# Where the blocks of x are added up for the layer norms at the ends of out, att_out and pool_out

## The chip, the cores and the metric

One core of one Trainium2 chip runs the whole program. The metric is device microseconds from start to end of one execution; the times shown are the median, lowest and highest of three runs. Durations inside the program come from one profiled execution.

## The reference, cut to what matters

A token matrix x of 256 tokens by 1024 channels passes through two transformer-like blocks (a gated mixer with a state-space branch and a squared-ReLU MLP; then attention, a pooling mixer and four gated MLPs). Eight times the new x is formed from a matrix product and normed before the next stage:

```
x = x + g1 * (mixed @ w_out)                       # "out", then h2 = rms_norm(x) * (1 + sc2) + sh2
x = x + g2 * (square(relu(h2 @ w_ff1)) @ w_ff2)    # "ff2", then rms_norm(x, final_norm_w)
x = layer_norm(ALPHA * x + 0.5 * swiglu(x) @ down)  # "down0", "down1", "down2", "down3"
x = layer_norm(ALPHA * x + attention(x) @ w_out)    # "att_out"
x = layer_norm(ALPHA * x + pool_mixer(x) @ w_out)   # "pool_out"
```

layer_norm needs the mean and the mean square over the 1024 channels of each token, rms_norm the mean square alone.

## The kernel before, in words

All data is fp32. x lies transposed in SBUF (tile `XS`): eight blocks of 128 channels by 256 tokens, each beside its square (`xb` is the x half, `sq` the square half), so `XS[:, m, :, :]` is 128x512. Weights come as 1 MB panels of 128x2048 into four slots of `raw`, by a DMA from SP's queue (`refill`), which waits until VectorE has split the panel that lay there. A panel is split in two halves of 128x1024: ScalarE rounds it into `w_hi` (L1104), VectorE subtracts to get `w_lo` (L1504), two panels ahead of TensorE. A product is then three matmuls (w_lo by the rounded operand, w_hi by the operand's rest, w_hi by the rounded operand: L601, L603, L604).

Each of the stages above has two groups of four output blocks. VectorE takes a block up out of PSUM and makes the new x of it (`new_x`: L1565 in out and ff2, L1560 elsewhere); ScalarE squares it (four blocks at once at L1156 for the first group, one by one at L1112 for the last). The last group is finished bank by bank (`each=bank_done`), so that its four takes can follow the matmuls closely (`last_group`, `bank_post`).

For the norm TensorE multiplies by a constant matrix `mean_w` of 1/1024, which sums over the partitions; the eight blocks are added up beforehand as far as possible. GpSimd adds blocks 0 to 4, with their squares, into `part` (`add_first_group`, L567: four adds), VectorE adds block 5 (`add_block`, L1573) ahead of the take of block 7, its last, and TensorE takes blocks 6 and 7 by themselves (`stats`, L747 to L757: three matmuls for the mean, three for the mean square; out and ff2 have only the last three). VectorE then computes the variance (L1618, or L1621 without a mean), ScalarE the inverse root, and the normed blocks `H` are made one by one for the next stage's first products (`apply_norm`, with two half-panel splits in between).

The order on each engine is the order of the code. Stages with 8 input blocks go through `run`: in out and pool_out VectorE and ScalarE split both halves of the next stage's first panel before the last group's takes. att_out is written out by hand: a loop over 14 half panels (`for i in range(14)`) splits, among others, the first panel of gu1 in its last two turns, then the takes of both groups follow.

## Time and profile before

| | us |
| --- | --- |
| median of 3 runs | 1671.67 |
| lowest, highest | 1669.38, 1672.41 |
| the profiled execution | 1670.81 |
| its span, first to last instruction | 1668.9 |
| TensorE matmul busy | 1584.6 (95%) |
| VectorE busy | 997.2 (60%) |
| ScalarE busy | 770.9 (46%) |
| GpSimd busy | 185.7 (11%) |

The profiled execution took 1.9 us more than its span. "PE" is TensorE's matmuls, DVE VectorE, ACT ScalarE, POOL GpSimd, SPq the queue from which SP issues DMAs. In a timeline a row gives the start, the duration, the engine, the line, the operation with output and inputs, how many were merged into the row, and in brackets how long the engine had been idle before and what it waited for. In a row of windows come the stretch and its length, the busy time of TensorE's matmuls, its weight loads, VectorE, ScalarE and GpSimd, and then the granted clock of TensorE (1.00 is 2.4 GHz, 0.50 is 1.2 GHz, between them a mean of both), the DMA share and GB/s. The mean granted clock over the span is 0.968.

### The profile page before, as it was taken

Reading aid. Unit: us, or ns where it says so; the run is one execution under the profiler, and the core shown is the slowest. Engines: PE = TensorE matmul, PEld = TensorE weight load, DVE = VectorE, ACT = ScalarE, POOL = GpSimd, SP = SyncE. Lnnn points to the kernel's source line nnn. Section 1 sums busy time; section 2 is a strip of 40 time slices with the busy share of each in tenths; the row PEclk is TensorE's granted clock in tenths of the full one; section 3 lists DMA queues with packets and bytes.
Section 4 is the critical chain, followed back from the end, with each engine's and each line's share of the span. In section 5 each row is a group of like instructions: output and inputs, shape, how many; then the busy total and the mean of one; then the engine's idle time right before and its main releaser. Section 6 shows DMA issues by size and latency. Waiting matters only on the chain.

```text
span 1668.9 us, 30136 instructions
## 1 busy us (share of the span) xinstructions
PE 1584.6 (95%) x12512; PEld 1534.6 (92%) x12512; DVE 997.2 (60%) x1278; ACT 770.9 (46%) x1006; POOL 185.7 (11%) x143
## 2 busy tenths in 40 slices
PE   7999999988999999999999879999999997799997
PEld 5999998878989999999989679999899997799997
DVE  5876894345766645655465655555655558565545
ACT  3544555444455534544443545443544444354433
POOL 0100002332110001000022012001200013120001
PEclk9999999989999999999999989999999998899999
DMA  8964763222535555455535325554455543344550
GB/s 316 368 246 165 292 229 124 102 77 102 185 145 179 191 185 177 163 190 176 187 141 189 114 79 200 178 194 181 151 179 187 190 177 127 126 152 176 180 192 32
DMA packets 42153, 289.66 MB, mean 174 GB/s; under 512 B 4843, under 2 KB 7019, under 8 KB 7500
## 3 DMA queue, kind: packets, MB, share of 16 engines
q1 hardware_dynamic: 41244, 284.44, 46.9%
q0 software_dynamic: 816, 3.87, 0.6%
q8 instruction: 72, 1.18, 0.3%
q14 instruction: 21, 0.17, 0.0%
HBM read 285.15 MB, written 3.15 MB: 173 GB/s over the span
## 4 chain that ended last, share of the span: by engine, by line
PE 86%; DVE 6%; ACT 3%; issue 2%; POOL 1%; DMA 1%; SPq 0%; ACTq 0%; POOLq 0%; DVEq 0%
PE banks L601 21%; PE banks L603 21%; PE banks L604 20%; PE banks L702 6%; PE banks L704 6%; PE banks L705 6%; DVE w_lo L1504 2%; ACT w_hi L1104 1%; POOL part L567 1%; PE banks L916 0%; PE banks L733 0%; PE banks L827 0%; DMA raw<-in_panels 0%; PE banks L919 0%; PE banks L826 0%
## 5 line engine op out<-in xcount | busy, mean ns | idle before, releaser
L1504 DVE TENSOR_TENSOR w_lo<-raw,w_hi 128x1024 fp32r<-128x1024 f32 x490 | 614.5, 1263 | 532.1 <-ACT w_hi L1104 526.9
L1104 ACT ACTIVATE w_hi<-raw 128x1024 fp32r<-128x1024 f32 x490 | 515.4, 1057 | 578.7 <-PE banks L604 421.4
L601 PE MATMUL banks<-H,w_lo 128*128 128x256 f32 x1920 | 549.5, 286 | 29.6 <-DVE H L1644 20.1
L603 PE MATMUL banks<-H,w_hi 128*128 128x256 f32 x1920 | 548.3, 286 | 0.0
L604 PE MATMUL banks<-H,w_hi 128*128 128x256 f32 x1920 | 546.6, 285 | 0.0
L601 PEld LDWEIGHTS banks<-H,w_lo 128*128 128x128 f32 x1920 | 368.7, 192 | 32.8 <-issue 32.3
L604 PEld LDWEIGHTS banks<-H,w_hi 128*128 128x128 f32 x1920 | 369.1, 192 | 0.0
L603 PEld LDWEIGHTS banks<-H,w_hi 128*128 128x128 f32 x1920 | 369.1, 192 | 0.0
L603 PE MATMUL banks<-HH,w_hi 128*128 128x256 f32 x960 | 270.8, 282 | 0.0
L601 PE MATMUL banks<-HH,w_lo 128*128 128x256 f32 x960 | 270.6, 282 | 0.0
L604 PE MATMUL banks<-HH,w_hi 128*128 128x256 f32 x960 | 270.1, 281 | 0.0
L702 PE MATMUL banks<-H,w_lo 128*128 128x256 f32 x640 | 188.3, 294 | 3.8 <-DVE H L1707 3.6
L704 PE MATMUL banks<-H,w_hi 128*128 128x256 f32 x640 | 185.4, 290 | 0.0
L705 PE MATMUL banks<-H,w_hi 128*128 128x256 f32 x640 | 185.1, 289 | 0.0
L604 PEld LDWEIGHTS banks<-HH,w_hi 128*128 128x128 f32 x960 | 181.0, 189 | 0.0
L603 PEld LDWEIGHTS banks<-HH,w_hi 128*128 128x128 f32 x960 | 180.8, 188 | 0.0
L601 PEld LDWEIGHTS banks<-HH,w_lo 128*128 128x128 f32 x960 | 180.7, 188 | 0.0
L702 PEld LDWEIGHTS banks<-H,w_lo 128*128 128x128 f32 x640 | 125.9, 197 | 6.4 <-issue 6.0
L704 PEld LDWEIGHTS banks<-H,w_hi 128*128 128x128 f32 x640 | 126.0, 197 | 0.0
L705 PEld LDWEIGHTS banks<-H,w_hi 128*128 128x128 f32 x640 | 125.7, 196 | 0.0
L567 POOL TENSOR_TENSOR part<-XS 128x512 f32<-128x512 f32 x8 | 10.3, 1289 | 904.4 <-issue 582.8
L1134 ACT ACTIVATE HH<-ev 128x512 f32 (+2 forms) x52 | 36.3, 698 | 80.6 <-DVE ev L1549 67.8
(285 smaller groups left out, 1706.5 us busy)
## 6 DMA issues: line engine op xcount, KB each, us to landing
raw<-in_panels SPq DMA_DIRECT2D x269, 1024.0 KB, 4.8
bias_rows<-rev POOLq DMA_DIRECT2D x1, 2048.0 KB, 16.9
XS<-in_x_t SPq DMA_DIRECT2D x1, 1024.0 KB, 6.6
near<-bias_rows POOLq DMA_DIRECT2D x8, 128.0 KB, 2.8
out_t<-XS SPq DMA_DIRECT2D x4, 256.0 KB, 2.6
ws<-in_ws_t POOLq DMA_DIRECT2D x1, 512.0 KB, 9.3
cols<-in_cols SPq DMA_DIRECT2D x1, 180.0 KB, 2.4
wdt<-in_wdt POOLq DMA_DIRECT2D x1, 128.0 KB, 5.9
```

Source lines behind the costliest of these rows:

```text
L567: pool.tensor_tensor(total, XS[:, 0, :, :] if b == 1 else total, XS[:, b, :, :], ALU.add)\
L601: pe.matmul(acc, w_lo[:, panel_slot, at:at + P], operand[:, kk, 0, :], start=starts and c == chunks[0], stop=False)
L603: pe.matmul(acc, w_hi[:, panel_slot, at:at + P], operand[:, kk, 1, :], start=False, stop=False)
L604: return pe.matmul(acc, w_hi[:, panel_slot, at:at + P], operand[:, kk, 0, :], start=False, stop=stops and c == chunks[-1])
L702: pe.matmul(acc, w_lo[:, q % SPLIT, at:at + P], operand[:, k, 0, :], start=p == 0 and c == 0 and b % 2 == 0, stop=False)
L704: pe.matmul(acc, w_hi[:, q % SPLIT, at:at + P], operand[:, k, 1, :], start=False, stop=False)
L705: last = pe.matmul(acc, w_hi[:, q % SPLIT, at:at + P], operand[:, k, 0, :], start=False, stop=p == panels - 1 and c == 3 and b % 2 == 1)
L1104: act.activation(w_hi[:, sl, w], raw[:, r, w], ACT.Copy).then_inc(panel_hi, 1)
L1134: act.activation(view[:, g, :, :], ev[:, G, 0:blocks, :], ACT.Copy).then_inc(operand_hi, 1)
L1504: vec.tensor_tensor(w_lo[:, sl, w], raw[:, r, w], w_hi[:, sl, w], ALU.subtract).then_inc(panel_lo, 1)
```

## The change

At three of the eight ends (out, att_out, pool_out) GpSimd no longer adds; VectorE adds all of blocks 1 to 5 to block 0. `SUMMED_AHEAD` names the five other ends, where GpSimd's adds stay.

- out and pool_out: VectorE makes the first three adds right behind the first group's takes (each waits for the one before it), splits only half 0 of the next panel, takes two blocks, adds block 4, takes, adds block 5, takes the last block, and then splits half 1.
- att_out: VectorE's loop has 12 turns in place of 14, so the two halves of gu1's first panel are split behind the last take and the last add. The first group's takes release ScalarE one by one (`x_early`), and ScalarE squares them one by one. The adds stand between the last group's takes, that of block 5 behind the last.
- TensorE, at all ends but att_out: the product with `part` comes first, ahead of blocks 6 and 7. At att_out it comes behind them, but ahead of the square of block 7.
- ScalarE's splits, and the order of the DMAs, are not moved.

VectorE's rows at the end of att_out. L1504 (before) and L1524 (after) are the splits, L1560 and L1583 the takes, L1573 and L1598 the adds, L1608 and L1652 the first step of the norm. Before:

```order
L1504 TENSOR_TENSOR w_lo<-raw,w_hi 128x1024
L2003 TENSOR_TENSOR AO<-banks,AO 128x256 x2
L1504 TENSOR_TENSOR w_lo<-raw,w_hi 128x1024 x2
L1560 SCALAR_TENSOR_TENSOR XS<-XS,banks 128x256 x7
L1573 TENSOR_TENSOR part<-part,XS 128x512
L1560 SCALAR_TENSOR_TENSOR XS<-XS,banks 128x256
L1608 TENSOR_TENSOR XS<-XS,banks 128x256
```

After:

```order
L2044 TENSOR_TENSOR AO<-banks,AO 128x256 x2
L1583 SCALAR_TENSOR_TENSOR XS<-XS,banks 128x256 x5
L1598 TENSOR_TENSOR part<-XS 128x512
L1598 TENSOR_TENSOR part<-part,XS 128x512
L1583 SCALAR_TENSOR_TENSOR XS<-XS,banks 128x256
L1598 TENSOR_TENSOR part<-part,XS 128x512
L1583 SCALAR_TENSOR_TENSOR XS<-XS,banks 128x256
L1598 TENSOR_TENSOR part<-part,XS 128x512
L1583 SCALAR_TENSOR_TENSOR XS<-XS,banks 128x256
L1598 TENSOR_TENSOR part<-part,XS 128x512
L1524 TENSOR_TENSOR w_lo<-raw,w_hi 128x1024 x2
L1652 TENSOR_TENSOR XS<-XS,banks 128x256
```

The two splits went from ahead of the eight takes to behind them, and five adds stand where one was.

VectorE's rows at the end of pool_out (out has the same order). Before:

```order
L1560 SCALAR_TENSOR_TENSOR XS<-XS,banks 128x256 x4
L1504 TENSOR_TENSOR w_lo<-raw,w_hi 128x1024 x2
L1560 SCALAR_TENSOR_TENSOR XS<-XS,banks 128x256 x3
L1573 TENSOR_TENSOR part<-part,XS 128x512
L1560 SCALAR_TENSOR_TENSOR XS<-XS,banks 128x256
L1608 TENSOR_TENSOR XS<-XS,banks 128x256
```

After:

```order
L1583 SCALAR_TENSOR_TENSOR XS<-XS,banks 128x256 x4
L1598 TENSOR_TENSOR part<-XS 128x512
L1598 TENSOR_TENSOR part<-part,XS 128x512 x2
L1524 TENSOR_TENSOR w_lo<-raw,w_hi 128x1024
L1583 SCALAR_TENSOR_TENSOR XS<-XS,banks 128x256 x2
L1598 TENSOR_TENSOR part<-part,XS 128x512
L1583 SCALAR_TENSOR_TENSOR XS<-XS,banks 128x256
L1598 TENSOR_TENSOR part<-part,XS 128x512
L1583 SCALAR_TENSOR_TENSOR XS<-XS,banks 128x256
L1524 TENSOR_TENSOR w_lo<-raw,w_hi 128x1024
L1652 TENSOR_TENSOR XS<-XS,banks 128x256
```

Three adds stand ahead of the split, two between the takes, and one half of the split went behind the last take.

TensorE's rows for the statistics of down0 (down1, down2, down3 and pool_out have the same). `part` is the sum of blocks 0 to 5. Before:

```order
L747 MATMUL banks<-XS,mean_w 128x256
L749 MATMUL banks<-XS,mean_w 128x256
L751 MATMUL banks<-part,mean_w 128x256
L753 MATMUL banks<-XS,mean_w 128x256
L755 MATMUL banks<-part,mean_w 128x256
L757 MATMUL banks<-XS,mean_w 128x256
```

After:

```order
L753 MATMUL banks<-part,mean_w 128x256
L759 MATMUL banks<-XS,mean_w 128x256
L761 MATMUL banks<-XS,mean_w 128x256
L753 MATMUL banks<-part,mean_w 128x256
L767 MATMUL banks<-XS,mean_w 128x256
L772 MATMUL banks<-XS,mean_w 128x256
```

The product with `part` went from third place to first, so that behind the take of block 7 (which L749 and L761 wait for) four matmuls follow and no longer five.

The diff, cut to its core:

```diff
@@ -94,2 +94,5 @@
 
+
+SUMMED_AHEAD = tuple(n for n in NORMED if n not in ("out", "att_out", "pool_out"))
+
 COUNTED = {
...
@@ -557,2 +560,3 @@
                 k = n - 2
+                done = BANKS * SUMMED_AHEAD.index(NORMED[k])
                 pool.wait_ge(taken, FIRST_GROUP[INDEX[NORMED[k]]] + 1)
...
@@ -563,3 +567,3 @@
                     if b > 1:
-                        pool.wait_ge(S["norm_part"], 4 * k + b - 1)
+                        pool.wait_ge(S["norm_part"], done + b - 1)
                     if b >= BANKS:
...
@@ -580,3 +582,4 @@
                         .then_inc(S["pool_lo_wide"], 1)
-                add_first_group(4 + i)
+                if NORMED[i + 2] in SUMMED_AHEAD:
+                    add_first_group(4 + i)
 
...
@@ -744,15 +747,27 @@
                     mean_at, square_at = banks[:, b, 0:T], banks[:, b + 1, 0:T]
+                    late = stage == "att_out"
+
+                    def whole(at, i, start):
+
+                        pe.wait_ge(S["norm_whole"], k + 1)
+                        return pe.matmul(at, mean_w[:, :], part[:, i, :], start=start, stop=i == 0 and not start)
+
                     pe.wait_ge(bank_x, (BANKS - 1) * (k + 1))
                     if mean:
-                        pe.matmul(mean_at, mean_w[:, :], xb[:, KD - 2, :], start=True, stop=False)
+                        if not late:
+                            whole(mean_at, 0, True)
+                        pe.matmul(mean_at, mean_w[:, :], xb[:, KD - 2, :], start=late, stop=False)
                         pe.wait_ge(taken, FIRST_GROUP[INDEX[stage] + 1])
-                        pe.matmul(mean_at, mean_w[:, :], xb[:, KD - 1, :], start=False, stop=False)
-                        pe.wait_ge(S["norm_whole"], k + 1)
-                        pe.matmul(mean_at, mean_w[:, :], part[:, 0, :], start=False, stop=True)                            .then_inc(S["mean_sum"], 1)
+                        last = pe.matmul(mean_at, mean_w[:, :], xb[:, KD - 1, :], start=False, stop=not late)
+                        if not late:
+                            last.then_inc(S["mean_sum"], 1)
+                    if not late:
+                        whole(square_at, 1, True)
                     pe.wait_ge(S["squares"], KD * n + KD - 1)
-                    pe.matmul(square_at, mean_w[:, :], sq[:, KD - 2, :], start=True, stop=False)
-                    pe.wait_ge(S["norm_whole"], k + 1)
-                    pe.matmul(square_at, mean_w[:, :], part[:, 1, :], start=False, stop=False)
+                    pe.matmul(square_at, mean_w[:, :], sq[:, KD - 2, :], start=late, stop=False)
+                    if late:
+                        whole(mean_at, 0, False).then_inc(S["mean_sum"], 1)
+                        whole(square_at, 1, False)
                     pe.wait_ge(S["squares"], KD * (n + 1))
-                    pe.matmul(square_at, mean_w[:, :], sq[:, KD - 1, :], start=False, stop=True)                        .then_inc(S["stat_sums"], 1)
+                    pe.matmul(square_at, mean_w[:, :], sq[:, KD - 1, :], start=False, stop=True).then_inc(S["stat_sums"], 1)
                     return
...
@@ -1467,4 +1482,9 @@
                     exps(h)
-            for g in range(2):
-                squares_post(INDEX["att_out"], g, (att_group + g) % 2)
+            for b in range(BANKS):
+                if b < BANKS - 1:
+                    act.wait_ge(S["x_early"], b + 1)
+                else:
+                    act.wait_ge(taken, FIRST_GROUP[INDEX["att_out"]] + 1)
+                act.activation(sq[:, b, :], xb[:, b, :], ACT.Square).then_inc(S["squares"], 1)
+            squares_post(INDEX["att_out"], 1, 1 - att_group)
             layer_norm("att_out")
...
@@ -1572,3 +1595,9 @@
                 vec.wait_ge(S["squares"], KD * (k + 2) + m + 1)
-                vec.tensor_tensor(part[:, :, :], part[:, :, :], XS[:, m, :, :], ALU.add).then_inc(S["norm_whole"], 1)
+                if m == 1:
+                    vec.wait_ge(S["stat_sums"], k + 2)
+                ins = vec.tensor_tensor(part[:, :, :], XS[:, 0, :, :] if m == 1 else part[:, :, :], XS[:, m, :, :], ALU.add)
+                if m == 5:
+                    ins.then_inc(S["norm_whole"], 1)
+                else:
+                    step(ins)
 
...
@@ -1576,7 +1605,17 @@
 
-                for b in range(BANKS):
-                    if b == BANKS - 1:
-                        vec.wait_ge(S["norm_part"], 4 * NORMED.index(name) + 4)
-                        add_block(name, 5)
-                    bank_post(INDEX[name], g, G, b, new_x)
+                alone = name in SUMMED_AHEAD
+                adds = {3: (5,)} if alone else {1: (1, 2), 2: (3,), 3: (4,), 4: (5,)} if name == "att_out" else {2: (4,), 3: (5,)}
+                for b in range(BANKS + 1):
+                    if b == BANKS - 1 and alone:
+                        vec.wait_ge(S["norm_part"], BANKS * SUMMED_AHEAD.index(name) + BANKS)
+                    for m in adds.get(b, ()):
+                        add_block(name, m)
+                    if b < BANKS:
+                        bank_post(INDEX[name], g, G, b, new_x)
+
+            def split_but_last(name):
+
+                def split_some(q, *place, halves=(0, 1)):
+                    split(q, *place, halves=(0,) if q == FIRST_PANEL[INDEX[name] + 1] else halves)
+                return split_some
 
...
@@ -1589,2 +1628,4 @@
                         last_group(name, g, G, new_x)
+                        if name not in SUMMED_AHEAD:
+                            split_half(FIRST_PANEL[s + 1], 1)
                         return
...
@@ -1594,3 +1635,6 @@
                     last.then_inc(taken, 1)
-                run(vec, INDEX[name], split, take_up)
+                    if name not in SUMMED_AHEAD:
+                        for m in (1, 2, 3):
+                            add_block(name, m)
+                run(vec, INDEX[name], split if name in SUMMED_AHEAD else split_but_last(name), take_up)
 
...
@@ -2005,3 +2046,3 @@
 
-            for i in range(14):
+            for i in range(12):
                 q, half = att_half(i)
...
@@ -2017,5 +2058,6 @@
             for b in range(BANKS):
-                last = deep_x(b, banks[:, NEAR + b // 2, b % 2 * T:b % 2 * T + T])
-            last.then_inc(taken, 1)
+                deep_x(b, banks[:, NEAR + b // 2, b % 2 * T:b % 2 * T + T]).then_inc(taken if b == BANKS - 1 else S["x_early"], 1)
             last_group("att_out", 1, 1 - att_group, deep_x)
+            split_half(att_half(12)[0] + SPLIT, 0)
+            split_half(att_half(12)[0] + SPLIT, 1)
             layer_norm("att_out", 1)
```

## Rows read from the trace of the kernel before

**Rows 1.** The page: the chain that ended last, by engine.

```profile
PE 86%; DVE 6%; ACT 3%; issue 2%; POOL 1%; DMA 1%; SPq 0%; ACTq 0%; POOLq 0%; DVEq 0%
```

**Rows 2.** Timeline of TensorE, end of att_out (start us, us, engine, line).

```profile
979.82 0.28 PE L604 MATMUL banks<-AO,w_hi 128*128 128x256 f32 x1
...
989.35 0.61 PE L757 MATMUL banks<-XS,mean_w 128*128 128x256 f32 x2
993.38 0.55 PE L601 MATMUL banks<-H,w_lo 128*128 128x256 f32 x1 [3.42 <-DVE H L1644]
```

**Rows 3.** Timeline of VectorE there.

```profile
975.53 1.23 DVE L1504 TENSOR_TENSOR w_lo<-raw,w_hi 128x1024 fp32r<-128x1024 f32 x1 [1.56 <-ACT w_hi L1104]
976.68 2.46 DVE L1560 SCALAR_TENSOR_TENSOR XS<-XS,banks 128x256 f32<-128x256 f32 x7
984.70 0.69 DVE L1573 TENSOR_TENSOR part<-part,XS 128x512 f32<-128x512 f32 x1 [5.57 <-POOL part L567]
985.31 0.41 DVE L1560 SCALAR_TENSOR_TENSOR XS<-XS,banks 128x256 f32<-128x256 f32 x1
...
990.00 0.42 DVE L1618 SCALAR_TENSOR_TENSOR st<-banks,st 128x256 f32<-128x256 f32 x1 [1.27 <-PE banks L757]
```

**Rows 4.** Timeline of GpSimd there.

```profile
980.72 3.95 POOL L567 TENSOR_TENSOR part<-part,XS 128x512 f32<-128x512 f32 x3
```

**Rows 5.** Timeline of VectorE at the end of down0.

```profile
857.83 0.42 DVE L1560 SCALAR_TENSOR_TENSOR XS<-XS,banks 128x256 f32<-128x256 f32 x1 [0.40 <-PE banks L604]
```

**Rows 6.** Timeline of TensorE there.

```profile
857.51 0.28 PE L604 MATMUL banks<-HH,w_hi 128*128 128x256 f32 x1
...
859.71 0.59 PE L755 MATMUL banks<-part,mean_w 128*128 128x256 f32 x2
860.14 0.59 PE L757 MATMUL banks<-XS,mean_w 128*128 128x256 f32 x2
```

**Rows 7.** Timeline of ScalarE at the end of att_out.

```profile
974.44 1.06 ACT L1104 ACTIVATE w_hi<-raw 128x1024 fp32r<-128x1024 f32 x1 [1.72 <-PE banks L1020]
...
979.26 1.28 ACT L1151 ACT_TABLE_LOAD   x1
980.55 1.03 ACT L1112 ACTIVATE XS<-XS 128x256 f32<-128x256 f32 x3
```

**Rows 8.** Timeline of VectorE, three adds in a chain, each waiting for the last.

```profile
224.84 2.32 DVE L1680 SCALAR_TENSOR_TENSOR part<-raw,c_r,part 128x512 f32<-128x512 f32 x3
```

**Rows 9.** Timeline of TensorE at the end of out.

```profile
471.79 0.29 PE L604 MATMUL banks<-MX,w_hi 128*128 128x256 f32 x1
...
474.51 0.70 PE L757 MATMUL banks<-XS,mean_w 128*128 128x256 f32 x2
```

**Rows 10.** Timeline of VectorE there.

```profile
466.62 3.77 DVE L1504 TENSOR_TENSOR w_lo<-raw,w_hi 128x1024 fp32r<-128x1024 f32 x2 [2.14 <-ACT w_hi L1104]
...
473.53 0.48 DVE L1565 SCALAR_TENSOR_TENSOR XS<-banks,mod,XS 128x256 f32<-128x256 f32 x1
```

**Rows 11.** Timeline of ScalarE there, the first group.

```profile
464.58 1.06 ACT L1156 ACTIVATE XS<-XS 128x1024 f32<-128x1024 f32 x1 [2.92 <-DVE XS L1565]
```

**Rows 12.** Timeline of TensorE at the end of pool_out.

```profile
1456.03 0.28 PE L604 MATMUL banks<-H,w_hi 128*128 128x256 f32 x1
...
1459.95 0.59 PE L757 MATMUL banks<-XS,mean_w 128*128 128x256 f32 x2
```

**Rows 13.** Timeline of VectorE there.

```profile
1457.65 0.41 DVE L1560 SCALAR_TENSOR_TENSOR XS<-XS,banks 128x256 f32<-128x256 f32 x1
```

**Rows 14.** Windows from a stage's first products: busy us, then PEclk.

```profile
478.20:486.20 8.00, 7.90 (x44) 7.93 (x45) 7.49 (x15) 4.08 (x8) 0.00 (x0) 0.63 0.13 32
...
993.40:1001.40 8.00, 8.00 (x55) 7.85 (x56) 8.00 (x18) 3.90 (x7) 0.00 (x0) 0.83 0.07 14
```

**Rows 15.** Timeline of SP's queue behind the splits of gu1's first panel.

```profile
976.94 0.33 SPq L474 DMA_DIRECT2D raw<-in_panels  x1
```

**Rows 16.** Timeline of ScalarE, first split of gu1's fifth panel.

```profile
1010.96 1.04 ACT L1104 ACTIVATE w_hi<-raw 128x1024 fp32r<-128x1024 f32 x1
```

More of the change, by code:

```diff
@@ L286, in two_blocks @@
             "v_folded x_folded rel_hi rel_split v_log mod_used mod_summed mod_rowed mod_turned mod_taken ws_loaded dt_got silu_done mix_sum "
-            "norm_whole stat_log mean_sum squares stat_sums stat_var stat_root stat_mean norm_part norm_centred norm_y norm_hi norm_lo norm_x "
+            "norm_whole stat_log mean_sum x_early squares stat_sums stat_var stat_root stat_mean norm_part norm_centred norm_y norm_hi norm_lo norm_x "
             "ident_r_ready "
@@ L568, in add_first_group @@
                         .then_inc(S["norm_part"], 1)
-            add_first_group(2)
             pool.wait_ge(half_used, 2 * FIRST_PANEL[INDEX["ff1"]])
@@ L1504, in split, with split_half @@
                     vec.tensor_tensor(w_lo[:, sl, w], raw[:, r, w], w_hi[:, sl, w], ALU.subtract).then_inc(panel_lo, 1)
+            def split_half(q, half):
+                split(q, *raw_place(q), halves=(half,))
             def products_done(s, g):
@@ L1694, in mod_column @@
                 ins.then_inc(S["mod_taken"], 1)
-            def split_half(q, half):
-                split(q, *raw_place(q), halves=(half,))
             def x_normed(blocks):
```

## The prediction

> **What bounds the kernel now.** I read the chain of waits first. It runs on TensorE for 86% of the span [rows 1], so time is won where TensorE stands still: at the eight ends, between a stage's last product and the next stage's first. Then I read the timelines of att_out's end. TensorE's last product starts at 979.82, the next stage's first at 993.38 [rows 2]: 13.6 us. The reader is to see why: VectorE idles 5.57 us until GpSimd's adds are done and only then makes its own add (984.70) and takes block 7 (985.31) [rows 3]; GpSimd's last three adds run from 980.72 to 984.67 [rows 4]. From the take on it is a fixed chain: last statistics matmul at 989.35, variance at 990.00, first product 3.38 us behind that.
>
> When could VectorE have taken block 7? At down0, where GpSimd was in time, the take starts 0.32 us behind the start of the last product (857.51, 857.83) [rows 5, 6]. I use this 0.32 at all ends.
>
> **att_out.** Before, both splits of gu1's first panel stood ahead of the takes; the first take came at 976.68, behind the split of 975.53 [rows 3], though ScalarE's wait for the same products was over at 974.44 [rows 7]. Without the splits VectorE takes from 974.44, every 0.34 us (seven in 2.46, the last 0.41), until 975.87.
>
> ScalarE still rounds its half first (974.44 to 975.50), so its four squares end by about 976.9 at 0.34 each [rows 7]; VectorE's first add needs the square of block 1, at about 976.1. Bank by bank the products end 1.43 us apart (12 of the 0.12 us steps), so the last group can be taken at 975.87, 977.29, 978.71 and 980.14 (979.82 + 0.32). An add of 128x512 takes 0.69 on VectorE, and what follows it starts 0.61 behind its start [rows 3]. A chain in which each add waits for the one before costs 0.035 more than its own length (three of 0.75 in 2.32) [rows 8]: 0.72 a piece. Two adds from 976.2 to 977.6, take, add (to 978.65), take at 978.71, add 979.1 to 979.8, take at 980.14. The add of block 4 needs ScalarE's square behind its table load (1.28 us [rows 7]): 976.9 + 1.28 + 0.34 = 978.5, in time. So the take of block 7 moves from 985.31 to 980.14.
>
> Behind it, VectorE still has the add of block 5 (starts 980.48) and the two splits it had pushed back, 1.15 each from start to start [rows 3]: 980.48 + 0.61 + 2.30 = 983.39. The first step of the norm adds 0.34, so the variance starts at 983.73. TensorE is earlier: its product with part starts at about 981.5, the last statistics matmul two steps of 0.43 later (859.71 to 860.14) [rows 6], 982.3, and its sum is there 0.65 later (989.35 to 990.00), at 983.0. VectorE's splits are therefore late next, by 0.7 us. Gain: 990.00 - 983.73 = **6.27 us**. TensorE's statistics also run at full clock rather than at half, which is in this number.
>
> The splits are queued ahead of the variance, and that is what costs the 0.7. The Trainium skill says so too ("TensorE: Matmul & The Clock Gate", section "Architectural detail: the array is 16× 32×32, not 1× 128×128"): VectorE's queue is strict FIFO. By that rule the gain here is 6.27; if the variance could pass the splits it would be 7.0. The rows show no instruction passing another on VectorE.
>
> **out.** The last product starts at 471.79 [rows 9], so the last take can start at 472.11 rather than at 473.53 [rows 10]. The first three adds start behind ScalarE's square of the first group (464.58 + 1.06, so about 465.7 [rows 11]) and end by 467.9; half 0's split takes 1.23 (the 3.77 for two [rows 10] was beside GpSimd's adds, now gone), to 469.1; two takes and the add of block 4 follow, until about 470.7. Block 6 can be taken 1.43 before block 7, at 470.68; 0.4 later the add of block 5 starts, until 471.8: ready 0.3 before 472.11. The last statistics matmul follows the take by 0.98 (473.53 to 474.51) and needs the square of block 7, as before. Half 1's split runs from 472.5 to 473.7, the sums are there at 473.8: hidden, with 0.1 us to spare. Gain: **1.42 us**.
>
> **pool_out.** Last product 1456.03 [rows 12], take at 1456.35 rather than 1457.65 [rows 13]. Block 6 is taken 1.43 earlier, at 1454.92, the add of block 5 starts 0.34 later and ends at 1455.95, 0.2 before TensorE could use it. So TensorE's six statistics matmuls stand in a row from 1456.15 every 0.43, the last at 1458.30 rather than 1459.95. Half 1's split ends at 1457.9, before the norm can begin at 1458.0. Gain: **1.65 us**.
>
> **The four down ends.** Here only TensorE's order changes. Before, the sixth matmul came at 860.14, and the first can start at 857.51 + 0.12 = 857.63. With part's product first, which is ready by then, nothing waits in between: 857.63 + 5 x 0.43 = 859.78. Gain 0.36 each, **1.44 us** for four. Counting matmuls behind the take (four and no longer five) gives 0.43 each; I take the smaller. ff2 has no mean and keeps its last wait, the square of block 7: nothing.
>
> **The clock.** Behind each end TensorE starts at half clock (1.2 of 2.4 GHz) for a while, with its own products waiting. In the eight microseconds from the first product the time at half is 8 x 2 x (1 - c): 5.9 us at out (c = 0.63), 2.7 at att_out (0.83) [rows 14]. The seven starts are of two kinds: two long (out and down0, 0.63 and 0.64), five short (0.79 to 0.83, 3.2 us on average). Half of that is lost: 3.0 us for a long one, 1.6 for a short one. I take each start to be drawn anew once everything has moved; at odds of two in seven that adds nothing on average. But at att_out TensorE will stand idle 4.2 us, from 982.9 (the last statistics matmul's end) to 987.1 (983.73 + 3.38), where it stood 3.4 before; for that I charge 0.3.
>
> The Trainium skill speaks against such gaps (same page, section "HAM oscillation — how this bites in real kernels"): idle stretches between bursts throttle the array again, and half of the throttled time is lost. The trace agrees: all seven starts here, each behind an idle stretch, show a granted clock below 1. By that rule the longer gap at att_out makes the long kind likelier there; what that would give is the first rival below.
>
> **The costs that the trace doesn't show.** The adds on VectorE whose two inputs are both blocks of XS: from 0.42 (a 128x256 take) to 1.23 (a 128x1024 split) [rows 3, 5]; I take 0.69, the same operation and shape. At 1.23 the adds would be late by about 2.3 us at each of the three ends (five adds 0.54 longer, less 0.3 to 0.4 of slack), and 3.6 of the gain would be left. At 0.42 att_out gains 0.27 more. ScalarE's four squares for one: ends at four times 0.34, or four times 0.42 at worst, 0.3 later, which moves att_out's first adds but not its last take, which has 0.3 of slack.
>
> **The sum.** 6.27 + 1.42 + 1.65 + 1.44 - 0.3 = 10.5 us. The profiled execution took 1670.81, so 1660.3. The median of the runs, 1671.67, lies 0.9 above that execution; I leave this to the range. The three runs differ by 3.0 us, and about 0.2% (3.3 us) is what a measurement of this kernel can tell from no change.
>
> **The rivals.**
> *The clock takes part of it back.* The starts behind att_out and pool_out turn long as out's is. For it: TensorE's longer idle time at att_out, and that both are short now. Against it: five of seven are short. Price 1.6 at att_out and 1.4 at pool_out, less the 0.3 counted: 1663.0.
> *The clock gives more.* out's and down0's starts turn short, 1.4 each: 1657.5. For it: two of seven are long now, and out's idle stretches grow shorter. Against it: nothing in the rows says what decides the kind.
> *The end of att_out only partly closes.* GpSimd isn't the only reason if the squares of the first group reach VectorE late: then the chain of adds ends behind 980.14, and with adds as long as a split the whole change is worth 3.6 us, 1667.2. For it: five adds and four takes in 6 us leave 0.3 us of slack. Against it: the duration of the same add, eight times 0.69.
> *Slower.* The pushed-back splits free gu1's panel slot late. SP issued its refill at 976.94, right behind the split [rows 15]; it will come at 983.5. If the panel were not there when ScalarE wants it, every later panel would be late in turn. ScalarE first wants it at 1010.96 [rows 16], 6.3 earlier in the new kernel: 1004.7. That leaves 21 us for the load. Beyond those 21 us each us of delay is lost; 32 us would cost all of the 10.5 won, and at 34 the time is 1672.8. Against it: the same load is covered before by 34 us (976.94 to 1010.96), and the issue moves by 6.6 only; out's slot moves by 3.
> *It doesn't do what it says*: the ends close but another engine sets the pace right behind, so that nothing comes out: 1670.8. Against it: behind each start TensorE is busy 7.9 to 8.0 of 8 us [rows 14].
>
> **How the numbers follow.** Forecast 0.68; clock takes 0.12; clock gives 0.10; partly closed 0.06; no effect 0.02; slower 0.02. The forecast's own range is 2 us either way. The range takes in both clock cases, and half of the way to the partly closed one: 1656.6 to 1664.6. Faster by over 0.2% (below 1668.4) holds for all but no effect, slower and a third of the partly closed: 0.94; same 0.04; slower 0.02.
>
> **What would show it.** In the profile after: no VectorE wait on GpSimd at these ends; at att_out the take of block 7 0.3 us behind the last product, the last statistics matmul about 2.5 us behind that product, both splits between the last add and the norm, and the first product 7.3 us behind the last one instead of 13.6. From the last product's start to the last statistics matmul's, out should show 1.3 us instead of 2.7, pool_out 2.3 instead of 3.9, the down ends 2.3 instead of 2.6. It would be wrong if the adds on VectorE took over 0.8, if a wait on ScalarE's squares stood ahead of them at the last take, or if att_out's stretch stayed above 9 us.

## The result and the profile after

The changed kernel ran in 1658.80 us (median of 4, 1655.21 to 1662.20) against 1672.04 for the kernel before on the same chip: ratio 0.9924, 95% interval 0.9900 to 0.9948, 12.7 us faster. A second comparison on another chip (c_after below) gave 1657.79 against 1669.45: ratio 0.9933, interval 0.9910 to 0.9957, 11.2 us. The forecast was 1660.3 with a range of 1656.6 to 1664.6; it was right in sign and size. Here and below, a difference in us is one minus the ratio, times the median of the kernel before in the same comparison.

The profiled execution took 1655.21 us with a span of 1653.4, mean granted clock 0.974. Its page has, where [rows 1] has 86% for TensorE:

```profile
PE 1575.2 (95%) x12512; PEld 1527.8 (92%) x12512; DVE 1002.9 (61%) x1290; ACT 771.0 (47%) x1009; POOL 165.3 (10%) x131
PE 88%; DVE 6%; ACT 3%; issue 2%; DMA 1%; POOL 0%; SPq 0%; ACTq 0%; DVEq 0%; POOLq 0%
```

GpSimd is busy 20 us less, 19 of them in these adds (53.3 to 34.5), and VectorE only 6 us more: the 12 adds take 0.69 each there, and splits that ran beside GpSimd's adds are shorter now (at out two took 3.77 before, 1.23 and 1.22 after). TensorE's share of the chain rises because it stands still less.

Each end can be measured as one stretch, from the start of a stage's last product to the first product of the next stage (for down3, to the last instruction):

| us | out | ff2 | down0 | att_out | down1 | down2 | pool_out | down3 | sum |
| --- | --- | --- | --- | --- | --- | --- | --- | --- | --- |
| before | 6.51 | 4.94 | 6.63 | 13.55 | 6.63 | 6.64 | 7.92 | 13.42 | 66.24 |
| after | 5.09 | 4.94 | 6.31 | 7.30 | 6.31 | 6.30 | 6.38 | 13.08 | 55.72 |
| won | 1.42 | 0 | 0.32 | 6.25 | 0.32 | 0.34 | 1.54 | 0.34 | 10.5 |
| forecast | 1.42 | 0 | 0.36 | 6.27 | 0.36 | 0.36 | 1.65 | 0.36 | 10.8 |

The largest one, att_out, on VectorE in the timeline of the changed kernel (answers to [rows 3]):

```profile
969.78 1.78 DVE L1583 SCALAR_TENSOR_TENSOR XS<-XS,banks 128x256 f32<-128x256 f32 x5 [4.09 <-PE banks L1035]
971.48 0.68 DVE L1598 TENSOR_TENSOR part<-XS 128x512 f32<-128x512 f32 x1
972.20 0.69 DVE L1598 TENSOR_TENSOR part<-part,XS 128x512 f32<-128x512 f32 x1
...
975.49 0.42 DVE L1583 SCALAR_TENSOR_TENSOR XS<-XS,banks 128x256 f32<-128x256 f32 x1 [0.40 <-PE banks L607]
975.82 0.68 DVE L1598 TENSOR_TENSOR part<-part,XS 128x512 f32<-128x512 f32 x1
976.42 2.35 DVE L1524 TENSOR_TENSOR w_lo<-raw,w_hi 128x1024 fp32r<-128x1024 f32 x2
978.70 0.41 DVE L1652 TENSOR_TENSOR XS<-XS,banks 128x256 f32<-128x256 f32 x1
```

At the last take VectorE waits for nothing but TensorE's own last product now: the take at 975.49 names PE L607, where before a 5.57 us wait on GpSimd stood. The adds take 0.68 to 0.69, and a chained one starts 0.72 behind the one before it (971.48, 972.20), as the forecast had taken. The two splits are done at 978.70, and only then does the norm begin. TensorE and ScalarE at the same end (answer to [rows 2, 7]):

```profile
975.10 0.28 PE L607 MATMUL banks<-AO,w_hi 128*128 128x256 f32 x1
...
977.79 0.59 PE L772 MATMUL banks<-XS,mean_w 128*128 128x256 f32 x2
982.40 0.55 PE L604 MATMUL banks<-H,w_lo 128*128 128x256 f32 x1 [4.01 <-DVE H L1688]
```

```profile
977.56 0.38 ACT L1189 ACTIVATE st<-banks 128x256 f32<-128x256 f32 x1 [1.20 <-PE banks L753]
```

The last statistics row starts 2.69 behind the last product, where it was 9.53. ScalarE has read the sum at 977.94, and VectorE comes to it at 978.70: its splits are 0.76 late, forecast 0.7. TensorE stands idle 4.01, forecast 4.2.

pool_out on TensorE (answer to [rows 12]), the whole list behind the last product:

```profile
1444.45 0.28 PE L607 MATMUL banks<-H,w_hi 128*128 128x256 f32 x1
1444.59 0.67 PE L753 MATMUL banks<-part,mean_w 128*128 128x256 f32 x2
1445.09 0.59 PE L759 MATMUL banks<-XS,mean_w 128*128 128x256 f32 x2
...
1446.82 0.59 PE L772 MATMUL banks<-XS,mean_w 128*128 128x256 f32 x2
1450.83 0.36 PE L604 MATMUL banks<-H,w_lo 128*128 128x256 f32 x1 [3.42 <-DVE H L1688]
```

The six stand in a row, the last 2.37 behind the last product, before 3.92. The first step is 0.50 and not 0.43 (1444.59 to 1445.09); with the 0.02 by which the first one comes later than taken, that is most of the 0.11 missing here. At out and down0 the same measure went from 2.72 to 1.31 and from 2.62 to 2.30.

SP's refill of the slot (answer to [rows 15]) comes at 978.96, behind the pushed-back splits, and no wait on a DMA shows at ScalarE's or VectorE's splits up to 1100:

```profile
978.96 10.17 SPq L477 DMA_DIRECT2D raw<-in_panels  x2
```

### The profile page after: what moved, and what is told of

The parts are those of the page before. It is cut to its first block, busy times and chain, and to the rows that moved or that the text cites. A ratio compares the mean times of both kernels' runs of the same rounds, so it can differ in the third digit from the quotient of the medians.

```text
span 1653.4 us, 30149 instructions
## 1 busy us (share of the span) xinstructions
PE 1575.2 (95%) x12512; PEld 1527.8 (92%) x12512; DVE 1002.9 (61%) x1290; ACT 771.0 (47%) x1009; POOL 165.3 (10%) x131
## 4 chain that ended last, share of the span: by engine, by line
PE 88%; DVE 6%; ACT 3%; issue 2%; DMA 1%; POOL 0%; SPq 0%; ACTq 0%; DVEq 0%; POOLq 0%
PE banks L604 21%; PE banks L607 21%; PE banks L606 21%; PE banks L705 6%; PE banks L707 6%; PE banks L708 6%; DVE w_lo L1524 2%; ACT w_hi L1119 1%; PE banks L931 0%; PE banks L736 0%; DMA raw<-in_panels 0%; PE banks L842 0%; PE banks L934 0%; DVE XS L1680 0%; PE banks L841 0%
## 5 line engine op out<-in xcount | busy, mean ns | idle before, releaser
L1524 DVE TENSOR_TENSOR w_lo<-raw,w_hi 128x1024 fp32r<-128x1024 f32 x490 | 612.2, 1258 | 518.5 <-ACT w_hi L1119 513.1
L607 PE MATMUL banks<-H,w_hi 128*128 128x256 f32 x1920 | 546.2, 284 | 0.0
L607 PEld LDWEIGHTS banks<-H,w_hi 128*128 128x128 f32 x1920 | 367.6, 191 | 0.0
L607 PE MATMUL banks<-HH,w_hi 128*128 128x256 f32 x960 | 270.1, 281 | 0.0
L607 PEld LDWEIGHTS banks<-HH,w_hi 128*128 128x128 f32 x960 | 180.7, 188 | 0.0
L571 POOL TENSOR_TENSOR part<-XS 128x512 f32<-128x512 f32 x5 | 6.5, 1292 | 756.5 <-issue 437.0
L590 POOL TENSOR_SCALAR XS<-XS,cols 128x256 f32<-128x256 f32 x40 | 58.1, 1471 | 217.6 <-DVE H L1688 217.6
```

The source lines that it names most:

```text
L571: pool.tensor_tensor(total, XS[:, 0, :, :] if b == 1 else total, XS[:, b, :, :], ALU.add)\
L590: pool.tensor_scalar(xb[:, m, :], xb[:, m, :], cols[:, at:at + 1], None, ALU.add)\
L607: return pe.matmul(acc, w_hi[:, panel_slot, at:at + P], operand[:, kk, 0, :], start=False, stop=stops and c == chunks[-1])
L1524: vec.tensor_tensor(w_lo[:, sl, w], raw[:, r, w], w_hi[:, sl, w], ALU.subtract).then_inc(panel_lo, 1)
```

## Experiments

The rival theories: (A) each edit closes its own wait, and the gains add up to the 10.5 of the stretches; (B) the adds alone carry att_out, and pushing the splits only costs 0.7; (C) the order on TensorE carries more than its 0.3 per end; (D) what stands above 10.5 comes from the clock. The lines in the diffs are against the changed kernel, and the diffs are cut to what matters.

**c_before and c_after: the two kernels, unchanged, once more,** to see what two traces of one program differ by.

> The kernel before once more, for a second trace. If the stretches at the ends are fixed by waits they repeat to 0.05 us (6.5, 4.9, 6.6, 13.6, 6.6, 6.6, 7.9), while the time at half clock behind them changes from end to end. If the 15.5 us between the two profiled spans were all due to the change, this span would be 1668.9 again; if some of it is spread between executions, the stages between the ends differ here too.

c_before took 1667.77, span 1665.7, where the first trace had 1668.9. Its stretches sum to 66.37 (66.24): they repeat within 0.03, but for out's, which is 6.62 here and 6.51 there. So 3.3 us came from outside the ends with the same program.

> The changed kernel once more, timed beside the two versions built on it and beside the kernel before. The stretches should repeat (5.1, 4.9, 6.3, 7.3, 6.3, 6.3, 6.4). The waits alone say 10.5 us below before; the first comparison had 12.7. If the 2.2 more belong to the change they show again; if they are the clock's draw they don't.

1657.79 (9 runs), as told above; span 1660.2 for the trace, stretches 55.68 (55.72). The stretches repeat within 0.02 at each end; the spans of these two traces differ by 6.8.

**e_att: att_out alone, with the new order on TensorE.**

```diff
-SUMMED_AHEAD = tuple(n for n in NORMED if n not in ("out", "att_out", "pool_out"))
+SUMMED_AHEAD = tuple(n for n in NORMED if n not in ("att_out",))
```

(and GpSimd's adds for out, which the changed kernel had dropped, are put back, here and in e_order)

> Of the change only att_out's end (VectorE's adds and the splits behind); GpSimd adds again at out and pool_out, and TensorE's product with part stays first everywhere but at att_out. If each end is worth its own wait, the stretch from the last product to the next stage's first is 7.3 us at att_out, 6.5 at out (as before) and 7.5 at pool_out, and the time lies 10.5 - 1.4 - 1.2 = 7.9 us below the kernel before. The rival, that the gain comes from the clock rather than from waits, expects the stretches to say little and the time to follow the time at half clock.

Ratio 0.9945 (0.9927 to 0.9964), 9.2 us faster. att_out is at 7.30, the down ends at 6.31, pool_out at 8.07 and out at 7.81, where the statistics ran at half clock in this trace; the sum of the stretches is 60.11, 6.1 less than before, at the lower end of the interval (6.0 to 12.2). out and pool_out are longer than the 6.5 and 7.5 expected: the product with `part` is first in the queue there and waits for GpSimd's sum (at out 1.81 us), as e_order shows in more detail.

**e_out_pool: out and pool_out alone.**

```diff
-SUMMED_AHEAD = tuple(n for n in NORMED if n not in ("out", "att_out", "pool_out"))
+SUMMED_AHEAD = tuple(n for n in NORMED if n not in ("out", "pool_out"))
...
-                    late = stage == "att_out"
+                    late = False
...
-            for i in range(12):
+            for i in range(14):
...
-            split_half(att_half(12)[0] + SPLIT, 0)
-            split_half(att_half(12)[0] + SPLIT, 1)
```

(and ScalarE's squares at att_out as before)

> Of the change only the ends of out and pool_out and TensorE's order; att_out as before but for part's product being first. Waits priced end by end: stretch 5.1 us at out, 6.4 at pool_out, about 13 at att_out; time 1.4 + 1.5 + 5 x 0.33 = 4.6 us below before. The rival (clock) expects the gain to be unrelated to the three stretches, anywhere from 2 to 9.

Ratio 0.9954 (0.9936 to 0.9971), 7.7 us faster. Stretches: out 5.09 and pool_out 6.38, both as in the changed kernel, so each end closes by itself. att_out takes 14.59, longer than before and than the 13 expected, with all six statistics products at half clock (1.06 us a row and more).

**e_order: only TensorE's order**, `SUMMED_AHEAD` with all names, the rest as in e_out_pool.

> Only TensorE's order: part's product first at all ends, GpSimd and VectorE as before. The waits say 0.33 us at each of the down ends, nothing at ff2, 0.4 at pool_out and a little at att_out (whose statistics run at half clock, so 0.8): about 2.5 us below before, that is hardly to be told from no change. If the order were the hidden cause of the 2 us won beyond the forecast, it would have to be 4 to 5 us.

Ratio 0.9983 (0.9965 to 1.0001), 2.8 us and not told from nothing. The down ends gain their 0.3, but the three ends where GpSimd is late lose: out 6.69 for 6.51, pool_out 8.08 for 7.92, att_out 14.11 for 13.55. I had not expected a loss. TensorE at att_out's end in this kernel:

```profile
983.87 1.19 PE L755 MATMUL banks<-part,mean_w 128*128 128x256 f32 x2 [5.43 <-DVE part L1595]
984.85 1.06 PE L761 MATMUL banks<-XS,mean_w 128*128 128x256 f32 x2
...
988.25 0.60 PE L774 MATMUL banks<-XS,mean_w 128*128 128x256 f32 x2
```

The first product with `part` waits 5.43 us, and the product of block 6, which was ready and used to fill the wait, is queued behind it and runs late. The first five of the six are at half clock (rows of 1.01 to 1.19 where pool_out's above are 0.59); in the kernel before four were. So part first is worth 0.3 only where part is there: the eight stretches sum to 65.82 for 66.24. C falls; in this change it could come first at out and pool_out only because the adds moved too.

**e_pushed: att_out with the splits behind, adds still on GpSimd.**

```diff
-SUMMED_AHEAD = tuple(n for n in NORMED if n not in ("out", "att_out", "pool_out"))
+SUMMED_AHEAD = tuple(n for n in NORMED if n not in ("out", "pool_out"))
```

(with `late = False` and ScalarE's squares as before; the loop stays at 12 turns)

> att_out alone differs from e_out_pool: the two splits stand behind the last take as in the changed kernel, but GpSimd still makes the adds of blocks 0 to 4. If the pushed-back splits alone were the gain, att_out's stretch would be 7.3 us. If GpSimd's 5.3 us of adds still bind, they start 2.3 us earlier (the takes do), the last take comes at 3.2 us behind the last product instead of 5.5, and the stretch is 10 to 11 us (9.5, and 1 more if TensorE's statistics fall to half clock).

One run, 1663.33; att_out 11.41. VectorE:

```profile
974.36 0.42 DVE L1578 SCALAR_TENSOR_TENSOR XS<-XS,banks 128x256 f32<-128x256 f32 x1 [1.00 <-PE banks L607]
978.22 0.69 DVE L1593 TENSOR_TENSOR part<-part,XS 128x512 f32<-128x512 f32 x1 [3.44 <-POOL part L571]
978.83 0.41 DVE L1578 SCALAR_TENSOR_TENSOR XS<-XS,banks 128x256 f32<-128x256 f32 x1
979.16 2.35 DVE L1519 TENSOR_TENSOR w_lo<-raw,w_hi 128x1024 fp32r<-128x1024 f32 x2
```

```profile
972.85 1.29 POOL L571 TENSOR_TENSOR part<-XS 128x512 f32<-128x512 f32 x1 [90.11 <-issue]
974.23 3.96 POOL L571 TENSOR_TENSOR part<-part,XS 128x512 f32<-128x512 f32 x3
```

The takes come early, and GpSimd alone is the wait: 3.44 us. Its adds are 1.3 each with VectorE idle or taking one block (1.29, then 3.96 for three), where VectorE needs 0.69. The last take comes 3.4 behind the last product (3.2 expected), and the stretch is 0.4 above the 10 to 11 expected.

**e_adds: att_out with VectorE's adds, splits still ahead.**

```diff
-            for i in range(12):
+            for i in range(14):
...
-            split_half(att_half(12)[0] + SPLIT, 0)
-            split_half(att_half(12)[0] + SPLIT, 1)
```

> att_out with VectorE's adds, but both splits of the next panel ahead of the takes again, all else as in the changed kernel. The takes start 2.3 us later, the chain of takes and adds ends with the take of block 7 about 1.9 us behind the last product (0.3 in the changed kernel), and no split stands ahead of the norm: stretch 8.2 us. If the adds moved to VectorE were all there is to the gain, it would be 7.3 or less (6.6 if the 0.7 us of the pushed-back splits were the only difference).

One run, 1659.12; att_out 8.38, for 8.2 expected. VectorE's adds and takes stand in one unbroken row from 971.59 and end late:

```profile
970.45 1.23 DVE L1524 TENSOR_TENSOR w_lo<-raw,w_hi 128x1024 fp32r<-128x1024 f32 x1 [1.56 <-ACT w_hi L1119]
971.59 1.74 DVE L1583 SCALAR_TENSOR_TENSOR XS<-XS,banks 128x256 f32<-128x256 f32 x5
...
976.81 0.42 DVE L1583 SCALAR_TENSOR_TENSOR XS<-XS,banks 128x256 f32<-128x256 f32 x1
977.14 0.69 DVE L1598 TENSOR_TENSOR part<-part,XS 128x512 f32<-128x512 f32 x1
979.30 0.42 DVE L1652 TENSOR_TENSOR XS<-XS,banks 128x256 f32<-128x256 f32 x1 [1.47 <-ACT st L1189]
```

So of the 6.25 won at att_out the adds, with ScalarE's squares and TensorE's order that go with them, bring 5.2 without the pushed splits (13.55 to 8.38). The pushed splits without the adds bring 2.1 (13.55 to 11.41), or 3.2 against e_out_pool, which has e_pushed's order on TensorE (14.59 to 11.41). Together they bring less than the sum, since both stand in the way of the same take. B was right that the adds carry most of it and wrong that pushing costs: it brings the last 1.1, with the 0.76 it costs behind the take already paid.

**e_half: one half of the split moved into the norm**, to win the 0.76.

```diff
                 for m in range(KD + 1):
+                    if m == 3 and stage_name == "att_out":
+                        split_half(att_half(12)[0] + SPLIT, 1)
...
-            split_half(att_half(12)[0] + SPLIT, 1)
             layer_norm("att_out", 1)
```

> The changed kernel, but at att_out only half 0 of the next panel is split ahead of the norm; half 1 follows behind the third normed block. If the splits hold the variance up by 0.7 us as the prediction has it, att_out's stretch falls from 7.3 to 6.6 us and TensorE does not wait for block 3 as long as it runs at half clock; at full clock it would wait up to 1 us there and win nothing. Time 0 to 0.7 us below the changed kernel, too little for the clock to show it in the total; the trace tells.

Ratio 0.9939 (0.9917 to 0.9960), 10.2 us faster than before, which isn't told from the changed kernel. The stretch did shrink, to 6.70: VectorE now waits for ScalarE and not the other way round (first fence). But the same 1.1 us of split sits further on, and TensorE, at full clock here, ran out of normed blocks behind 24 products (second fence).

```profile
978.37 1.22 DVE L1524 TENSOR_TENSOR w_lo<-raw,w_hi 128x1024 fp32r<-128x1024 f32 x1
979.92 0.42 DVE L1652 TENSOR_TENSOR XS<-XS,banks 128x256 f32<-128x256 f32 x1 [0.33 <-ACT st L1189]
...
985.36 2.35 DVE L1524 TENSOR_TENSOR w_lo<-raw,w_hi 128x1024 fp32r<-128x1024 f32 x2
```

```profile
983.74 0.36 PE L604 MATMUL banks<-H,w_lo 128*128 128x256 f32 x1 [3.41 <-DVE H L1688]
...
986.91 0.28 PE L607 MATMUL banks<-H,w_hi 128*128 128x256 f32 x1
988.98 0.36 PE L604 MATMUL banks<-H,w_lo 128*128 128x256 f32 x1 [1.79 <-DVE H L1688]
```

0.60 won in the stretch, 1.79 waited right behind it. The 0.76 of the splits is real in the stretch and free in the whole: from att_out's last product to down1's it is 197.2 us here and 197.5 in the changed kernel's first trace, whose start behind att_out was at half clock, but 196.7 in e_warm below, at full clock with both splits ahead.

**e_warm: the clock taken out.** Seven ends get idle products behind their last statistics product, 99 in all, with a result that nothing reads.

```diff
+FILL_IN = {"out": 13, "ff2": 13, "att_out": 17}
...
+                    if stage != "down3":
+                        for _ in range(FILL_IN.get(stage, 14)):
+                            pe.matmul(banks[:, b + 3, 0:P], mean_w[:, :], mean_w[:, :], start=True, stop=True)
```

> The changed kernel, and behind the statistics of seven ends 13 to 17 more matmuls of 128x128 on a constant into a free PSUM bank, that nobody reads (3 us of work in the 3.4 to 4.2 us in which TensorE would stand idle). If the time at half clock behind the ends comes from these idle stretches, it goes from 3 to 5.5 us at most ends to near 0, and the time falls by half of its sum (23.6 us in the changed kernel's trace): by about 10 us, to 1649. If it comes from something else, nothing changes; if the added matmuls delay the first products, the stretches grow by as much as they are late.

Ratio 0.9906 (0.9884 to 0.9928), 15.7 us faster than the kernel before: 1651.99. The stretches are those of the changed kernel within 0.02, and TensorE is at full clock at the first product of each. First att_out's end, then windows of 8 us behind the starts of out, down0 and att_out; the granted clock stands behind GpSimd's `(x0)`:

```profile
973.95 0.59 PE L773 MATMUL banks<-XS,mean_w 128*128 128x256 f32 x2
974.38 3.96 PE L776 MATMUL banks<-mean_w 128*128 128x128 f32 x34
978.56 0.36 PE L605 MATMUL banks<-H,w_lo 128*128 128x256 f32 x1 [0.22 <-DVE H L1692]
```

```profile
473.90:481.90 8.00, 7.60 (x60) 7.28 (x61) 7.48 (x15) 4.15 (x8) 0.00 (x0) 1.00 0.28 96
856.70:864.70 8.00, 7.23 (x55) 6.70 (x56) 8.00 (x18) 3.90 (x7) 0.00 (x0) 1.00 0.08 14
978.60:986.60 8.00, 7.25 (x55) 6.72 (x56) 8.00 (x18) 3.90 (x7) 0.00 (x0) 1.00 0.14 44
```

I had expected about 10 us from it, and it gave 3 to 5.5 (15.7 less the 12.7 and 11.2 of the changed kernel, or less e_half's 10.2 in the same comparison); the seven stages behind the ends are 3.7 us shorter together than in the changed kernel's first trace. The windows tell why: behind down0 and att_out TensorE is busy 7.2 of 8 us at full clock, VectorE all 8. TensorE then waits for the normed blocks (us in total over the trace, times, longest):

```profile
PE banks L605 <- DVE H L1692: 5.2, 12, 0.7
```

The mean granted clock is 0.977 to 0.983 in all six executions, and 0.967 to 0.974 in all 13 of the changed kernel, so the higher clock comes with the idle products. But idle time alone doesn't decide what a start gets: in e_order's trace, without any added products, five of the seven starts were at 1.00.

**e_warm_half: both,** with 14 idle products at att_out in place of 17.

> Both together: the added matmuls behind the statistics, and half 1 of the split behind the third normed block at att_out. Stretch 6.6 to 6.7 us at att_out, clock 1.00 behind the ends. The stretch is 0.6 us shorter, but at full clock TensorE needs block 3 earlier than at half clock and would wait for VectorE; if that wait eats the 0.6, the time equals that with the matmuls alone.

Ratio 0.9901 (0.9873 to 0.9930), 16.5 us faster, 1651.56: the lowest median of all, but not told from e_warm. att_out's stretch is 6.71, as expected. The clock is 1.00 at all seven starts, but not for long behind att_out: TensorE waits here for the same split as in e_half, and from then on the clock is at half for 3.4 us, which was not expected (the second fence is the window behind that wait):

```profile
978.96 0.46 PE L605 MATMUL banks<-H,w_lo 128*128 128x256 f32 x1 [1.80 <-DVE H L1692]
```

```profile
978.96:983.00 4.04, 4.04 (x21) 4.04 (x22) 4.04 (x10) 2.04 (x4) 0.00 (x0) 0.58 0.65 231
```

From att_out's last product to down1's it is 198.6 us, where e_warm has 196.7.

Over all executions of each kernel the mean span is 1650.1 for the 12 of these two and 1656.3 for the 13 of the changed kernel, with a standard deviation of some 3 us in each. So the idle products make a version that beats both kernels.

## Why the prediction was right, step by step

**The bound, right.** Time was to be won where TensorE stands still. The stretches lost 10.5 us, the whole 11 to 13.

**att_out, right: 6.25 for 6.27.** The take 0.4 behind the last product (forecast 0.3), the last statistics row 2.7 behind it (2.5), the splits late next, by 0.76 (0.7). The 0.2 by which the statistics were later than worked out is hidden behind the splits, as it was said that the splits would end last. The Trainium skill states that VectorE's queue is strict FIFO ("TensorE: Matmul & The Clock Gate", section "Architectural detail: the array is 16× 32×32, not 1× 128×128"). The trace agrees: the norm's first step starts at 978.70, right behind the two splits, with its sum there since 977.94, and in e_half, with one split ahead, it comes 1.6 behind the start of the splits in place of 2.3.

**out, exact: 1.42.** The last take starts 0.32 behind the last product, and TensorE's rows follow without a wait on GpSimd's sum:

```profile
469.67 0.28 PE L607 MATMUL banks<-MX,w_hi 128*128 128x256 f32 x1
469.91 0.67 PE L753 MATMUL banks<-part,mean_w 128*128 128x256 f32 x2
...
470.97 0.70 PE L772 MATMUL banks<-XS,mean_w 128*128 128x256 f32 x2
```

```profile
469.99 0.48 DVE L1588 SCALAR_TENSOR_TENSOR XS<-banks,mod,XS 128x256 f32<-128x256 f32 x1 [0.22 <-PE banks L607]
```

**pool_out 1.54 for 1.65, the down ends 0.32 to 0.34 for 0.36:** sizes off by 0.1 and 0.04, from the first step of the row, 0.50 for 0.43 at pool_out and 0.46 at down0:

```profile
852.87 0.62 PE L753 MATMUL banks<-part,mean_w 128*128 128x256 f32 x2
853.33 0.59 PE L759 MATMUL banks<-XS,mean_w 128*128 128x256 f32 x2
```

**The adds on VectorE, 0.68 to 0.69** as taken, from bounds of 0.42 and 1.23.

**The clock, mis-sized, and hidden by its small net.** The forecast knew two kinds of starts and charged half of the time at half clock: 3.0 and 1.6. The windows of the changed kernel (answers to [rows 14]) show three kinds:

```profile
859.10:867.10 8.00, 8.00 (x47) 8.00 (x48) 8.00 (x18) 3.90 (x7) 0.00 (x0) 0.66 0.09 14
982.40:990.40 8.00, 8.00 (x48) 8.00 (x49) 8.00 (x18) 3.90 (x7) 0.00 (x0) 0.69 0.21 57
1178.90:1186.90 8.00, 8.00 (x55) 8.00 (x56) 8.00 (x18) 3.90 (x7) 0.00 (x0) 0.81 0.05 8
1374.60:1382.60 8.00, 7.23 (x55) 6.71 (x56) 8.00 (x18) 3.89 (x7) 0.00 (x0) 1.00 0.07 14
```

At 0.81, which is 3.0 us at half clock, there are 55 matmuls in 8 us, and at 1.00 there are 55 as well: at full clock TensorE stands idle 0.77 us for VectorE's blocks, and the slow start only fills that. Here the prediction misread its rows: it took the 7.9 to 8.0 busy us of 8 behind a start [rows 14] as a sign that products were waiting and only the clock held them back. Part of those windows was at half clock, and at full clock the normed blocks come too slowly to keep TensorE busy. What a start costs can be read from the stage behind it, from its first product to its last:

| stage behind | no half clock | 2.8 to 3.4 us at half | 5.0 to 6.2 us at half |
| --- | --- | --- | --- |
| out | 183.07 (e_warm) | 183.73 (after) | 184.85 (before) |
| ff2 | 188.45 (e_warm) | 189.43 (before) | 190.67 (c_after) |
| att_out | 189.39 (e_warm) | 189.38 (before) | 190.16 (after) |

So the short kind costs 0 to 1.0 (charged 1.6), the long kind 0.8 to 2.2 (charged 3.0). The Trainium skill prices throttled time at half ("TensorE: Matmul & The Clock Gate", section "HAM oscillation — how this bites in real kernels"). No row of the table reaches that: the nearest are 2.2 of 6.2 behind ff2 and 1.8 of 5.9 behind out, and behind att_out nothing is lost for 2.8 us at half. As feared for att_out, its start did turn long in the profiled execution, 2.8 to 5.0 us at half, and that cost 0.8 there; in c_after the same start had 3.4 (that stage can't stand in the table, for the step told of below: 191.67). The first rival happened at att_out in one trace, at half its price.

**What stands above 10.5** (0.7 to 2.2 us): 10.5 lies inside both intervals, and two traces of the same program differ by more than what is left. A part of it is the clock, so D holds in part: out's start had 5.9 and 6.0 us at half in the two traces of the kernel before, and 3.4 in all six traces that have the new end at out and no idle products. The stage behind it took 184.85 and 184.91 in the kernel before and 183.73 and 183.75 in the changed one, 1.1 us less. Whether the shorter end makes that start short isn't shown. Much of what differs between two traces of one program lies ahead of out's last product, where the change has hardly begun: it comes at 469.67 in the first trace of the changed kernel and at 473.89 in c_after, 4.2 of their 6.8 us, with a granted clock of 0.96 and 0.94 in the first 465 us. Another part has a place too: in some executions a whole stage runs at a step of 0.1200 instead of 0.1187 between products, at a granted clock of 1.00 either way, which is 2 us in a stage of 190. The same 100 us in two traces of the kernel before, the first one and then c_before:

```profile
1500.00:1600.00 100.00, 100.00 (x836) 100.00 (x835) 54.03 (x53) 46.22 (x53) 0.00 (x0) 1.00 0.51 183
```

```profile
1500.00:1600.00 100.00, 100.00 (x845) 100.00 (x845) 54.77 (x54) 46.07 (x53) 0.00 (x0) 1.00 0.51 180
```

836 or 845 products in the same window, with TensorE busy throughout. The changed kernel shows it too: 845 between 1020 and 1120 in its first trace, 835 in c_after. What decides it stays open. Open too is e_out_pool: 7.7 us (4.8 to 10.7) where its stretches give 3.3, which the interval leaves out. Its stage behind out is 183.75, so the short start adds 1.1; what the stage behind down0 gains in its trace (114.61 for 115.68), the one behind ff2 loses (190.59 for 189.43), and the rest has no place.

**The rivals.** The clock takes part of it back: at att_out in the first trace, for 0.8 of the 1.6 charged, and not at pool_out (3.4 at half in both). The clock gives more: in part, out's start turned short in both traces, for 1.1 of the 1.4 charged; down0's stayed long in the first (5.5) and was short in c_after. Partly closed: out, the last takes at the three ends wait for nothing but TensorE's last product. Slower by a late refill: out, it came at 978.96 and nothing waited. No effect: out. That the sum came out near all the same owes something to luck: the terms of the ends were right, and the clock's gains and losses, each charged too high, were small in the net.

## What to carry to other kernels

When a serial end waits on two engines, find the moment at which each would be ready without the other: att_out closed only with the adds and the splits both out of the way (5.2 and 2.1 one without the other, 6.25 together), and a product moved to the front of a queue gains only where its operand is already there, or else everything ready behind it waits too. Check what the engine behind the gap does at full clock before pricing a slow start or a shortened gap: e_half's 0.6 and much of the clock's price were time in which TensorE would have waited for VectorE anyway. Measure repeated traces of one kernel, stretch by stretch; here the stretches repeat to 0.03 us, with one exception of 0.11, and the spans only to 7.

## What the runs showed of the hardware

- An add of 128x512 with both inputs in SBUF takes 1.3 us on GpSimd with VectorE idle or nearly so, 0.69 on VectorE (e_pushed). At out in the kernel before, beside VectorE's splits, GpSimd needed 5.74 for three.
- Idle products in the gaps kept the granted clock at 1.00 behind all seven ends, and the stage starts were at full clock (e_warm). Idle time alone doesn't decide it: five of seven starts in e_order's trace had 1.00 without them.
- Behind the norms, where TensorE waits for blocks even at full clock, time at half clock costs less than half of itself: 0 to 1.0 us for 2.8 to 3.4, 0.8 to 2.2 for 5.0 to 6.2.
- A product's step at a granted clock of 1.00 has two values, 0.1187 and 0.1200 us, each kept through a whole stage of an execution (845 and 836 products in 100 us).
